# Interleaving a token-mixing stage with the projections on either side of it, on one Trainium2 core

## The chip, the cores and the metric

The program runs on one core of one Trainium2 chip. The core has TensorE (PE, matmuls), VectorE (DVE), ScalarE (ACT), GpSimd (POOL) and SyncE (SP, which only issues transfers here). Each engine runs its own instruction list in order; engines wait for one another on semaphores. The metric is the device time in microseconds of one execution; smaller is better.

## What is computed

The reference is a chain of transformer layers on 256 tokens of width 1024. The part that the change touches is the second mixer, a gated MLP that mixes tokens within chunks of 128, and the first matmuls behind it:

```python
def gmlp_mixer(h, w_in, ln_g, ln_b, ws, bs, w_out):
    z = gelu(h @ w_in)                       # 1024 -> 4096
    u, v = z[..., :2048], z[..., 2048:]
    v = layernorm(v, ln_g, ln_b)
    vc = v.reshape(B, S // 128, 128, 8, 256) # chunks of 128 tokens, 8 groups of 256 features
    mixed = einsum('gpq,bnqgc->bnpgc', ws, vc) + bs.T[None, None, :, :, None]
    return (u * mixed.reshape(B, S, 2048)) @ w_out   # 2048 -> 1024
...
x = x + g_m * o_lat
x = x + g_f * squared_relu_mlp(modulate(x, norm_ffn_g[i], sh_f, sc_f), ffn_w1[i], ffn_w2[i])
```

## The kernel before

All engines' programs are written out by hand, with hand-placed semaphore waits; nothing reorders them. Activations lie feature-major: a tile is 128 features by 256 tokens.

**Split products.** Every large product is made of three matmuls (lines 529 to 531): a number is kept as a rounded high part and the rest as a low part, and high by high, low by high and high by low are summed in PSUM. So each weight chunk (128 by 1024, 512 KB, eight 128 by 128 tiles) passes ACT, which writes `w_hi` (line 1148), and then DVE, which writes `w_lo` (line 1579). Four chunks are held in a ring: `convert(c)` on ACT waits until PE has used chunk c - 4 (`matmul_steps`), `convert(c)` on DVE waits for ACT's (`weight_hi`), and PE waits for DVE's (`weight_lo`). Activations are split likewise: DVE makes an fp32 tile in one of four slots of `tile_f32`, ACT writes `s_hi`, POOL writes `s_lo` (line 2131).

**The stages around the change**, in PE's order:

- `gm_u0` (8 chunks): the first half of u. `gm_v` (16 chunks): v, with tokens on the partitions. `gm_u1` (8 chunks, 8 groups): the second half of u. A group is the 24 matmuls that fill one PSUM bank. Banks 0 and 1 alternate; ACT's Gelu (`evacuate`, line 1163) empties each.
- During `gm_u1` DVE converts seven chunks, normalises v (`ln_mv`, `v_gm`, line 1930, semaphore `v_normed`), makes 16 bias terms of 128 by 128 (line 1924), and does four of the products that make the conditioning vectors of later layers (`modulate_loop`, line 1594).
- Mixing: for each of 16 tiles t, PE multiplies `v_gm` by `ws` (line 881) into bank 4 or 5; DVE applies gain and bias (line 1941) and multiplies by u (line 1944); ACT and POOL split the result. PE's step t waits until DVE has read tile t - 2.
- `gm_out` (16 chunks): 8 groups of 16 tiles each, banks 0 and 1. DVE adds each group into the residual x (`residual`, line 1672); ACT scales x and rounds it (`raw_tile`), DVE makes the low part (`raw_low`, line 1645), ACT squares it. `ffn1_up` begins on these tiles, and its first group needs all eight.

Of the kernel before, what the change touches and what calls it, by code (L numbers as in the profile page):

```python
# [31 lines left out]
GM = 2048  # L32
# [20 lines left out]
    ("gm_u0", [1] * 8), ("gm_v", [0, 0, 0, 2] * 4), ("gm_u1", [1] * 8), ("gm_out", [0, 1] * 8),  # L53
# [48 lines left out]
def banks_of_groups(count):  # L102
# [44 lines left out]
def build_program(nc, vecs, consts, gm_rows, c_rows, rel_ext, x_in, ctx_in, ada, weights,  # L147
# [13 lines left out]
    with hold:  # L161
# [219 lines left out]
        class Attention:  # L381
# [14 lines left out]
        ln_counted, ln_var, ln_std, v_normed, ws_sums, ws_sum_ready, mixed = (  # L396
            sem(n) for n in ("ln_counted", "ln_var", "ln_std", "v_normed", "ws_sums", "ws_sum_ready", "mixed"))
# [125 lines left out]
        def _(pe):  # L523
# [350 lines left out]
            run(project("gm_u1", 8, normed))  # L874
            pe.wait_ge(v_normed, 2)
            pe.wait_ge(ws_sum_ready, 2)
            for t in range(GM // P):
                if t >= 2:
                    pe.wait_ge(split_src, written(split0["gm_s"] + t - 2))
                for n in range(2):  # L880
                    last = pe.matmul(bank[4 + t % 2][:, n * P:(n + 1) * P], v_gm[:, n, t * P:(t + 1) * P],  # L881
                                     ws[:, t // 2, :], start=True, stop=True)
                last.then_inc(mixed, 1)
# [255 lines left out]
        def _(act):  # L1139
# [423 lines left out]
        def _(dve):  # L1563
# [356 lines left out]
            dve.wait_ge(ws_sum_ready, 2)  # L1920
            dve.wait_ge(gm_in, 32)
            for j in range(7):
                for t in range(2 * j, 2 * j + (4 if j == 6 else 2)):
                    ins = dve.scalar_tensor_tensor((bs_all if t % 2 else mix_bias)[:, t // 2, :], ws_sum[:, t // 2, :],
                                                   V("gm_ln_b", t, 1), bs_all[:, t // 2, :], ALU.mult, ALU.add)
                convert(chunk0["gm_u1"] + j + 4)
# [7 lines left out]
            then(ins)  # L1934

            def mixed_tile(t):
                i = split0["gm_s"] + t
                dst = tile_f32[:, i % 4, :].rearrange("p (n q) -> p n q", n=2)
                dve.wait_ge(mixed, t + 1)
                dve.wait_ge(split_lo, i - 3)  # L1940
                then(dve.scalar_tensor_tensor(dst, bank[4 + t % 2][:, 0:S].rearrange("p (n q) -> p n q", n=2),
                                              V("gm_ln_g", t, 1),
                                              (bs_all if t % 2 else mix_bias)[:, t // 2:t // 2 + 1, :].to_broadcast([P, 2, P]), ALU.mult, ALU.add))
                dve.tensor_tensor(tile_f32[:, i % 4, :], tile_f32[:, i % 4, :], u_gm[:, t, :],
                                  ALU.mult).then_inc(split_src, 1)
# [181 lines left out]
        def _(pool):  # L2127
# [73 lines left out]
            pool.dma_start(sq[:, 4:8, :].rearrange("p a b -> p (a b)"), gm_rows.partition_broadcast(P)).then_inc(gm_in, 16)  # L2201
            for t in range(GM // P):
# [170 lines left out]
```

## Time and profile before

| what | value |
|---|---|
| median of 3 runs | 983.95 us (978.9 to 984.32) |
| the profiled execution, its own time | 983.29 us |
| its span | 981.5 us |
| mean granted TensorE clock | 0.973 |
| busy: PE, DVE, ACT, POOL | 935.3, 707.3, 539.3, 303.9 us |

Times inside the trace count from the start of the span. A busy share is a mean over very different stages; a stage is read from its own stretch.

### The profile page before, as it was taken

To read this page: it belongs to the slowest core of one execution; us is meant where nothing else is said; L and a number is where in the kernel's file an instruction comes from. 1 tells how busy PE (TensorE), PEld (TensorE's weight loads), DVE (VectorE), ACT (ScalarE), POOL (GpSimd) and SP (SyncE) were. 2 spreads that over 40 slices of the span, in tenths; PEclk is the share of its full clock that TensorE was granted. 3 is DMA by queue.
4 is the path that set the end of the run, shared out by engine and by line. 5 is a ranking of instruction groups with operands and counts; after the bars stand their busy time and mean duration, and the time that the engine had idled before them with its cause. 6 is when DMAs were issued, how large, how long until landed. Compare 5 with 4: busy or idle time off the path is not lost.

```text
span 981.5 us, 19551 instructions
## 1 busy us (share of the span) xinstructions
PE 935.3 (95%) x6882; PEld 869.0 (89%) x6882; DVE 707.3 (72%) x1134; ACT 539.3 (55%) x922; POOL 303.9 (31%) x272
## 2 busy tenths in 40 slices
PE   5998989899999999999979999999999999999996
PEld 5877557799999999988979999999999878899996
DVE  3997679777988777897976787555555873475664
ACT  3465656565665444655635666654444762674645
POOL 1952020137997111120052288731110000330012
PEclk9798999999999999999979999999999998999998
DMA  9856185169888777788615686555665332255421
GB/s 346 292 188 228 42 230 186 51 215 317 306 274 273 288 280 278 248 317 302 224 50 187 232 282 200 187 172 192 185 194 171 108 111 84 87 174 191 151 87 43
DMA packets 57052, 195.60 MB, mean 199 GB/s; under 512 B 6303, under 2 KB 9791, under 8 KB 56736
## 3 DMA queue, kind: packets, MB, share of 16 engines
q1 hardware_dynamic: 55312, 192.36, 57.9%
q0 software_dynamic: 1680, 2.44, 1.1%
q8 instruction: 37, 0.61, 0.3%
q14 instruction: 23, 0.19, 0.1%
HBM read 192.65 MB, written 1.07 MB: 197 GB/s over the span
## 4 chain that ended last, share of the span: by engine, by line
PE 77%; DVE 14%; issue 4%; ACT 3%; DMA 1%; POOL 0%; DVEq 0%; SPq 0%; ACTq 0%
PE bank L529 23%; PE bank L530 22%; PE bank L531 22%; DVE w_lo L1579 3%; DVE ada_raw L1586 2%; ACT w_hi L1148 1%; DVE products L1681 1%; PE bank L927 1%; PE bank L953 1%; PE bank L627 1%; DVE ada_raw L1681 1%; DMA x<-x_in 1%; PE bank L826 1%; PE bank L881 1%; DVE ada_raw L1594 1%
## 5 line engine op out<-in xcount | busy, mean ns | idle before, releaser
L1579 DVE TENSOR_TENSOR w_lo<-raw,w_hi 128x1024 fp32r<-128x1024 f32 (+1 forms) x261 | 338.8, 1300 | 107.3 <-ACT w_hi L1148 104.7
L1148 ACT ACTIVATE w_hi<-raw 128x1024 fp32r<-128x1024 f32 (+1 forms) x261 | 272.4, 1045 | 173.0 <-PE bank L531 165.1
L529 PE MATMUL bank<-act_hi,w_hi 128*128 128x258 f32 (+1 forms) x872 | 249.6, 286 | 0.0
L530 PE MATMUL bank<-act_lo,w_hi 128*128 128x258 f32 (+1 forms) x872 | 246.4, 283 | 0.0
L531 PE MATMUL bank<-act_hi,w_lo 128*128 128x258 f32 (+1 forms) x872 | 246.1, 282 | 0.0
L529 PEld LDWEIGHTS bank<-act_hi,w_hi 128*128 128x128 f32 x872 | 165.6, 190 | 3.3 <-issue 2.8
L530 PEld LDWEIGHTS bank<-act_lo,w_hi 128*128 128x128 f32 x872 | 165.6, 190 | 1.0 <-issue 1.0
L531 PEld LDWEIGHTS bank<-act_hi,w_lo 128*128 128x128 f32 x872 | 165.7, 190 | 0.0
L529 PE MATMUL bank<-hid_hi,w_hi 128*128 128x256 f32 x512 | 143.9, 281 | 0.0
L530 PE MATMUL bank<-hid_lo,w_hi 128*128 128x256 f32 x512 | 143.9, 281 | 0.0
L531 PE MATMUL bank<-hid_hi,w_lo 128*128 128x256 f32 x512 | 143.9, 281 | 0.0
L531 PEld LDWEIGHTS bank<-hid_hi,w_lo 128*128 128x128 f32 x512 | 97.2, 190 | 0.0
L529 PEld LDWEIGHTS bank<-hid_hi,w_hi 128*128 128x128 f32 x512 | 97.2, 190 | 0.0
L530 PEld LDWEIGHTS bank<-hid_lo,w_hi 128*128 128x128 f32 x512 | 96.1, 188 | 0.0
L2187 POOL TENSOR_TENSOR tile_f<-relu 128x256 f32<-128x256 f32 x64 | 80.4, 1256 | 30.6 <-ACT relu L1382 30.5
L2191 POOL TENSOR_TENSOR hid_lo<-tile_f,hid_hi 128x256 f32 x64 | 75.0, 1173 | 18.0 <-POOL tile_f L2187 18.0
L2139 POOL TENSOR_TENSOR square_sum<-square_sum,sq 128x256 f32<-128x256 f32 x30 | 38.8, 1292 | 134.6 <-ACT sq L1180 134.4
L1594 DVE CUSTOM_DVE_ANT_0 ada_raw<-ada_raw,silu_row 128x1024 f32<-128x1024 f32 x56 | 75.8, 1354 | 2.3 <-DMA ada_raw<-ada 2.0
L2131 POOL TENSOR_TENSOR s_lo<-tile_f,s_hi 128x256 fp32r<-128x256 f32 x24 | 23.4, 992 | 97.8 <-ACT s_hi L1153 97.8
L529 PE MATMUL bank<-s_hi,w_hi 128*128 128x256 f32 x192 | 53.5, 279 | 0.0
L530 PE MATMUL bank<-s_lo,w_hi 128*128 128x256 f32 x192 | 53.0, 276 | 0.0
L531 PE MATMUL bank<-s_hi,w_lo 128*128 128x256 f32 x192 | 53.0, 276 | 0.0
(356 smaller groups left out, 1820.4 us busy)
## 6 DMA issues: line engine op xcount, KB each, us to landing
raw<-weights SPq DMA_DIRECT2D x247, 512.0 KB, 3.8
ada_raw<-ada SPq DMA_DIRECT2D x88, 512.0 KB, 4.9
raw<-weights SPq DMA_DIRECT2D x14, 384.0 KB, 4.7
ada_more<-ada SPq DMA_DIRECT2D x8, 512.0 KB, 6.2
bias<-bias_by_distance SPq DMA_DIRECT2D x1, 2048.0 KB, 9.3
x<-x_in SPq DMA_DIRECT2D x1, 1024.0 KB, 7.5
ctx<-ctx_in SPq DMA_DIRECT2D x1, 1024.0 KB, 9.5
out<-result SPq DMA_DIRECT2D x4, 256.0 KB, 2.7
```

The source lines that it names most:

```text
L529: pe.matmul(dst, w[0], a[0], start=start, stop=False)
L530: pe.matmul(dst, w[0], a[1], start=False, stop=False)
L531: return pe.matmul(dst, w[1], a[0], start=False, stop=stop)
L1148: act.activation(w_hi[:, slot, 0:width_of(c)], raw[:, slot, 0:width_of(c)], ACT.Copy).then_inc(weight_hi, 1)
L1579: dve.tensor_tensor(w_lo[:, slot, 0:w], raw[:, slot, 0:w], w_hi[:, slot, 0:w].bitcast(fp32), ALU.subtract).then_inc(weight_lo, 1)
L1586: dve.tensor_tensor_reduce(ada_raw[:, a % RING, :], ada_raw[:, a % RING, :], silu_row[:], 1.0, V("ada_b0", 2 * KT + a, 1), ALU.mult, ALU.a ...
L1594: dve.tensor_tensor_reduce(ada_raw[:, q, :], ada_raw[:, q, :], silu_row[:], 1.0, 0.0, ALU.mult, ALU.add, ada_col[:, q:q + 1]).then_inc(ada ...
L1681: ins = dve.tensor_tensor_reduce(dst, first_ada(o), row[:], 1.0, V("ada_b0", k, 1), ALU.mult, ALU.add, mod_in[:, k, s_:s_ + 1])
L2131: pool.tensor_tensor(lo, tile_f32[:, i % 4, :], hi.bitcast(fp32), ALU.subtract).then_inc(split_lo, 1)
L2139: pool.tensor_tensor(square_sum[:], sq[:, 0, :] if k == 1 else square_sum[:], sq[:, k, :], ALU.add).then_inc(square_sums, 1)
L2187: pool.tensor_tensor(tile_f32[:, i % 4, :], relu[:, g % 2, :], relu[:, g % 2, :], ALU.mult).then_inc(hid_squared, 1)
L2191: pool.tensor_tensor(hid_lo[:, ds(it * 8 + g, 1), :], tile_f32[:, i % 4:i % 4 + 1, :], hid_hi[:, ds(it * 8 + g, 1), :].bitcast(fp32), ALU. ...
```

## The change

PE takes up `gm_u1` in three parts: groups 0 to 3; a wait for the normalised v; then groups 4 to 7 with one mixing tile behind each. Then each of the 16 input tiles of `gm_out` is used by two output groups at once (banks 2 and 3), with the mixing of tile k + 4 behind it; mixed tiles go through banks 4 to 7. The chunks of `w_out` are stored in the order that this needs. The other six groups follow, over four banks. The split tiles are kept in slots shifted by 8, since the inputs of `gm_u1` are still in use. POOL makes 8 of the 16 bias terms; DVE makes the low parts of tiles 2, 5, 8, 11 and 14 that POOL made. ACT's and DVE's lists are rewritten to match, and the two loops of `gm_out` are written out.

```diff
-("gm_out", [0, 1] * 8),
+("gm_out", [0, 0, 1, 1] + [0, 1] * 6),
...
+            elif name == "gm_out":
+                banks.append((g + 2) % 4)
...                                          # PE
-            run(project("gm_u1", 8, normed))
+            def mix(t):
+                if t >= 4:
+                    pe.wait_ge(split_src, written(split0["gm_s"] + t - 4))
+                for n in range(2):
+                    last = pe.matmul(bank[4 + t % 4][:, n * P:(n + 1) * P], v_gm[:, n, t * P:(t + 1) * P],
+                                     ws[:, t // 2, :], start=True, stop=True)
+                last.then_inc(mixed, 1)
+            def first_out(g, k):
+                n, c = group0["gm_out"] + g, chunk0["gm_out"] + 2 * (k // 8) + g
+                if k % 8 == 0:
+                    pe.wait_ge(weight_lo, c + 1)
+                if k == 0:
+                    pe.wait_ge(evacuated, n - 3)
+                last = split_product(bank[bank_of[n]][:, 0:S], weight(c, k % 8 * P, P), mixed_s(k), k == 0, k == 15)
+                if k % 8 == 7:
+                    last.then_inc(matmul_steps, 1)
+            stage = project("gm_u1", 8, normed)
+            for g in range(4):
+                next(stage)
             pe.wait_ge(v_normed, 2)
             pe.wait_ge(ws_sum_ready, 2)
-            for t in range(GM // P):
-                if t >= 2:
-                    pe.wait_ge(split_src, written(split0["gm_s"] + t - 2))
...
+            for t in range(4):
+                next(stage)
+                mix(t)
+            run(stage)
+            for k in range(GM // P):
+                pe.wait_ge(split_lo, split0["gm_s"] + k + 1)
+                first_out(0, k)
+                first_out(1, k)
+                if k + 4 < GM // P:
+                    mix(k + 4)
+            run(project("gm_out", 16, mixed_s, locals_=range(4, 16), banks=4))
...                                          # ACT, in the loop over the groups of gm_u1
+                if g >= 4:
+                    split(split0["gm_s"] + g - 4, s_hi[:, g + 4, :])
+            for t in range(4, GM // P):
+                split(split0["gm_s"] + t, s_hi[:, (t + KT) % 16, :])
+                if t == 7:
+                    shift_columns(SHIFT3)
+                if t in (10, 12):
+                    convert(chunk0["gm_out"] + t // 2 - 1)
             act.wait_ge(gains, 3)
+            for g in range(KT):
+                raw_tile("gm_out", g, gain_column(4))
+                for c in range(chunk0["gm_out"] + 2 * g + 6, chunk0["gm_out"] + min(2 * g + 8, 20)):
+                    convert(c)
+                square_residual("gm_out", g)
...                                          # DVE
+            for j in range(8):
+                if j < 7:
+                    convert(chunk0["gm_u1"] + j + 4)
                 if j in (1, 2):
                     dve.wait_ge(ln_std, j)
                     then(dve.reciprocal(ln_mv[:, j - 1, 3:4], ln_mv[:, j - 1, 2:3]))
...
                 if j % 2 == 0:
                     modulate_loop(68 + j // 2)
+                for i in range(j - 1, KT if j == 7 else j) if j > 0 else ():
+                    dve.wait_ge(mix_bias_ready, 2 * i + 2)
+                    then(dve.scalar_tensor_tensor(bs_all[:, i, :], ws_sum[:, i, :], V("gm_ln_b", 2 * i + 1, 1),
+                                                  bs_all[:, i, :], ALU.mult, ALU.add))
+                if j >= 4:
+                    mixed_tile(j - 4)
+                if j == 7:
+                    mixed_low(2)
+            for t in range(4, GM // P):
...
                 mixed_tile(t)
+                if t > 4 and t % 3 == 0:
+                    mixed_low(t - 1)
+                if t == 4:
+                    convert(chunk0["gm_out"] + 3)
+                if t == 7:
+                    gain_of(4, mods[:, SCALE3, :], V("norm_ffn_g", KT, KT))
+                if t in (11, 13):
+                    convert(chunk0["gm_out"] + (t - 3) // 2)
             shift_low(SHIFT3, 3)
+            for g in range(KT):
+                residual("gm_out", g, mods[:, GATE2, g:g + 1])
+                raw_low(RAW["ffn1_in"], g, gain_column(4))
+                for c in range(chunk0["gm_out"] + 2 * g + 6, chunk0["gm_out"] + min(2 * g + 8, 20)):
+                    convert(c)
...                                          # POOL
+            pool.wait_ge(ws_sum_ready, 2)
+            pool.wait_ge(gm_in, 32)
+            for j in range(GM // P // 2):
+                pool.tensor_scalar(mix_bias[:, j, :], ws_sum[:, j, :], V("gm_ln_b", 2 * j, 1), None,
+                                   ALU.mult).then_inc(mix_bias_ready, 1)
+                pool.wait_ge(mix_bias_ready, 2 * j + 1)
+                pool.tensor_tensor(mix_bias[:, j, :], mix_bias[:, j, :], bs_all[:, j, :], ALU.add).then_inc(mix_bias_ready, 1)
```

**PE, the end of `gm_u1` and the mixing.** Lines 529 to 531 before are 531 to 533 after, and 881 is 885; three rows are one input tile of a group. Before:

```order
L529 MATMUL bank1<-s_hi,w_hi 128x256
L530 MATMUL bank1<-s_lo,w_hi 128x256
L531 MATMUL bank1<-s_hi,w_lo 128x256
L881 MATMUL bank4<-ws,v_gm 128x128 x2
L881 MATMUL bank5<-ws,v_gm 128x128 x2
L881 MATMUL bank4<-ws,v_gm 128x128 x2
```

After, behind the last tile of `gm_u1` (bank 1):

```order
L533 MATMUL bank1<-s_hi,w_lo 128x256
L885 MATMUL bank7<-ws,v_gm 128x128 x2
L531 MATMUL bank2<-s_hi,w_hi 128x256
L532 MATMUL bank2<-s_lo,w_hi 128x256
L533 MATMUL bank2<-s_hi,w_lo 128x256
L531 MATMUL bank3<-s_hi,w_hi 128x256
L532 MATMUL bank3<-s_lo,w_hi 128x256
L533 MATMUL bank3<-s_hi,w_lo 128x256
L885 MATMUL bank4<-ws,v_gm 128x128 x2
```

The sixteen mixing steps stood in one block; now six matmuls of `gm_out` stand between two of them.

**ACT, from group 2 of `gm_u1` on.** `u_gm` is the emptying of a group, `w_hi` a weight chunk, `s_hi` the rounding of a mixed tile. Lines 1163, 1148 and 1153 before are 1192, 1177 and 1182 after. Before:

```order
L1163 ACTIVATE u_gm<-bank0 128x256
L1148 ACTIVATE w_hi<-raw 128x1024
L1163 ACTIVATE u_gm<-bank1 128x256
L1148 ACTIVATE w_hi<-raw 128x1024
L1163 ACTIVATE u_gm<-bank0 128x256
```

After, groups 4 to 6:

```order
L1192 ACTIVATE u_gm<-bank0 128x256
L1177 ACTIVATE w_hi<-raw 128x1024
L1182 ACTIVATE s_hi<-tile_f32 128x256
L1192 ACTIVATE u_gm<-bank1 128x256
L1177 ACTIVATE w_hi<-raw 128x1024
L1182 ACTIVATE s_hi<-tile_f32 128x256
L1192 ACTIVATE u_gm<-bank0 128x256
```

A rounding of a mixed tile, made by DVE, now stands between a chunk's conversion and the emptying of the next group.

**DVE, the same place.** `w_lo` is a weight chunk, `tile_f32` the two instructions of a mixed tile, `sq<-sq,vec` a bias term. Lines 1579, 1924, 1941 and 1944 before are 1611, 1983, 1958 and 1961 after. Before, the end of `gm_u1`:

```order
L1579 TENSOR_TENSOR w_lo<-raw,w_hi 128x1024
L1924 SCALAR_TENSOR_TENSOR mix_bias<-sq,vec 128x128
L1924 SCALAR_TENSOR_TENSOR sq<-sq,vec 128x128
L1579 TENSOR_TENSOR w_lo<-raw,w_hi 128x1024
L1594 ISA ada_raw,ada_col<-ada_raw,silu_row 128x1024
```

After, from the conversion that follows group 4 of `gm_u1`:

```order
L1611 TENSOR_TENSOR w_lo<-raw,w_hi 128x1024
L1626 ISA ada_raw,ada_col<-ada_raw,silu_row 128x1024
L1626 ISA ada_col 128x1
L1983 SCALAR_TENSOR_TENSOR sq<-sq,vec 128x128
L1958 SCALAR_TENSOR_TENSOR tile_f32<-bank4,vec,mix_bias 128x256
L1961 TENSOR_TENSOR tile_f32<-tile_f32,u_gm 128x256
L1611 TENSOR_TENSOR w_lo<-raw,w_hi 128x1024
L1983 SCALAR_TENSOR_TENSOR sq<-sq,vec 128x128
L1958 SCALAR_TENSOR_TENSOR tile_f32<-bank5,vec,sq 128x256
```

A mixed tile now stands behind a conversion, and the next conversion behind the tile; bank4 and bank5 are the first two of the four mixing banks.

**DVE, the last groups of `gm_out`.** `x` is the residual, `act_lo` the low part for `ffn1_up`. After, one group of the last seven:

```order
L1704 SCALAR_TENSOR_TENSOR x<-bank0,mods,x 128x256
L1677 SCALAR_TENSOR_TENSOR act_lo<-x,gain,act_hi 128x256
L1611 TENSOR_TENSOR w_lo<-raw,w_hi 128x1024 x2
```

Before, one conversion stood ahead of each residual and one behind it; now both stand behind one group's residual and ahead of the next one's.

## Rows read from the trace of the kernel before

**Rows 1.** The page, busy time of each engine.

```profile
PE 935.3 (95%) x6882; PEld 869.0 (89%) x6882; DVE 707.3 (72%) x1134; ACT 539.3 (55%) x922; POOL 303.9 (31%) x272
```

**Rows 2.** Busy time by stretch: most of `gm_u1`, then the mixing.

```profile
core 0: us, PE busy (x) PEld busy (x) DVE busy (x) ACT busy (x) POOL busy (x), PEclk, DMA share, GB/s
...
468.50:488.30 19.80, 19.80 (x177) 19.80 (x177) 18.92 (x37) 12.27 (x18) 0.00 (x0) 1.00 0.63 212
488.30:509.50 21.20, 14.47 (x78) 12.25 (x77) 19.18 (x41) 7.83 (x19) 13.22 (x15) 0.76 0.24 78
```

**Rows 3.** Timeline of PE's weight loads: start, length, what, idle before.

```profile
488.15 0.97 PEld L881 LDWEIGHTS bank<-ws,v_gm 128*128 128x128 f32 x8
492.56 1.78 PEld L881 LDWEIGHTS bank<-ws,v_gm 128*128 128x128 f32 x8 [3.44 <-DVE tile_f L1944]
...
508.01 0.19 PEld L529 LDWEIGHTS bank<-s_hi,w_hi 128*128 128x128 f32 x1
```

**Rows 4.** Waits, 440 to 570 us: total, times, longest.

```profile
PEld bank L881 <- DVE tile_f L1944: 8.9, 10, 3.4
```

**Rows 5.** Timeline of DVE in `gm_u1` and in the mixing.

```profile
474.67 0.34 DVE L1924 SCALAR_TENSOR_TENSOR sq<-sq,vec 128x128 f32<-128x128 f32 x1
474.93 1.21 DVE L1579 TENSOR_TENSOR w_lo<-raw,w_hi 128x1024 fp32r<-128x1024 f32 x1
...
479.37 1.35 DVE L1930 TENSOR_SCALAR v_gm<-v_gm,ln_mv 128x2048 f32<-128x2048 f32 x1
480.64 1.22 DVE L1594 CUSTOM_DVE_ANT_0 ada_raw<-ada_raw,silu_row 128x1024 f32<-128x1024 f32 x1
...
493.28 1.76 DVE L1579 TENSOR_TENSOR w_lo<-raw,w_hi 128x1024 fp32r<-128x1024 f32 x1
...
506.57 0.48 DVE L1941 SCALAR_TENSOR_TENSOR tile_f<-bank,vec,sq 128x256 f32<-128x256 f32 x1
...
507.45 0.48 DVE L1941 SCALAR_TENSOR_TENSOR tile_f<-bank,vec,mix_bias 128x256 f32<-128x256 f32 x1
...
509.24 0.71 DVE L1609 SCALAR_TENSOR_TENSOR gain<-mods,vec 128x8 f32<-128x8 f32 x1
```

**Rows 6.** Timeline of ACT in `gm_u1` and in the mixing.

```profile
476.58 0.39 ACT L1163 ACTIVATE u_gm<-bank 128x256 f32<-128x256 f32 x1
476.86 1.05 ACT L1148 ACTIVATE w_hi<-raw 128x1024 fp32r<-128x1024 f32 x1
477.81 0.37 ACT L1163 ACTIVATE u_gm<-bank 128x256 f32<-128x256 f32 x1
...
492.54 0.42 ACT L1153 ACTIVATE s_hi<-tile_f 128x256 fp32r<-128x256 f32 x1 [2.65 <-DVE tile_f L1944]
```

**Rows 7.** Timeline of POOL in the mixing.

```profile
493.04 2.58 POOL L2131 TENSOR_TENSOR s_lo<-tile_f,s_hi 128x256 fp32r<-128x256 f32 x2 [65.51 <-ACT s_hi L1153]
...
503.67 6.96 POOL L2131 TENSOR_TENSOR s_lo<-tile_f,s_hi 128x256 fp32r<-128x256 f32 x8 [0.81 <-ACT s_hi L1153]
```

**Rows 8.** Timeline of PE at the start of `ffn1_up`.

```profile
551.66 0.28 PE L529 MATMUL bank<-act_hi,w_hi 128*128 128x258 f32 x1
...
554.20 0.39 PE L529 MATMUL bank<-act_hi,w_hi 128*128 128x258 f32 x1
```

**Rows 9.** Timeline of DVE at the same place.

```profile
552.16 0.48 DVE L1672 SCALAR_TENSOR_TENSOR x<-bank,mods,x 128x256 f32 x1 [0.31 <-PE bank L531]
553.66 0.48 DVE L1645 SCALAR_TENSOR_TENSOR act_lo<-x,gain,act_hi  x1 [1.01 <-ACT act_hi L1174]
```

**Rows 10.** Busy time by stretch, around an earlier gap of PE (columns as in Rows 2).

```profile
90.00:93.00 3.00, 0.30 (x3) 0.21 (x2) 2.98 (x4) 1.03 (x2) 3.00 (x2) 0.91 0.93 369
93.00:95.00 2.00, 1.97 (x9) 1.97 (x10) 1.92 (x4) 0.07 (x1) 0.92 (x2) 0.50 1.01 361
...
99.00:101.00 2.00, 2.00 (x9) 1.59 (x9) 0.00 (x0) 0.13 (x1) 0.00 (x0) 0.93 0.47 193
```

**Rows 11.** Busy time by stretch, inside the mixing.

```profile
496.00:500.00 4.00, 3.66 (x15) 3.37 (x16) 2.97 (x7) 1.60 (x4) 2.76 (x4) 0.50 0.39 131
```

More of the change, by code:

```diff
@@ L52 @@
     ("ffn0_up", [1] * 32), ("ffn0_down", [0, 0, 0, 1] * 8),
-    ("gm_u0", [1] * 8), ("gm_v", [0, 0, 0, 2] * 4), ("gm_u1", [1] * 8), ("gm_out", [0, 1] * 8),
+    ("gm_u0", [1] * 8), ("gm_v", [0, 0, 0, 2] * 4), ("gm_u1", [1] * 8), ("gm_out", [0, 0, 1, 1] + [0, 1] * 6),
     ("ffn1_up", [1] * 32), ("ffn1_down", [0, 0, 0, 1] * 8),
@@ L873, in _, with mixed_s @@
                           stop=True).then_inc(ws_sums, 1)
-            run(project("gm_u1", 8, normed))
+            def mixed_s(k):
+                return s_hi[:, (k + KT) % 16, :], s_lo[:, (k + KT) % 16, :]
+            def mix(t):
[5 more added lines that the diff above has]
+                last.then_inc(mixed, 1)
@@ L875, in _ @@
+            for g in range(4):
+                next(stage)
             pe.wait_ge(v_normed, 2)
             pe.wait_ge(ws_sum_ready, 2)
-            for t in range(GM // P):
-                if t >= 2:
-                    pe.wait_ge(split_src, written(split0["gm_s"] + t - 2))
[L880 to L883, printed above, removed]
@@ L884, in _ @@
-            with pe.Fori(0, 2) as it:
-                run(project("gm_out", 16, lambda k: (s_hi[:, k, :], s_lo[:, k, :]), locals_=range(8),
-                            it=it, per=4, a_wait=lambda k: split0["gm_s"] + k + 1))
+            for t in range(4):
[8 more added lines that the diff above has]
+                    mix(k + 4)
@@ L1919, in _, with mixed_tile, mixed_low @@
                 dve.bn_aggr(ln_mv[:, tt, 0:2], ln_stats[:, tt, :, :]).then_inc(ln_var, 1)
[L1920 to L1926, printed above, removed]
+            def mixed_tile(t):
+                i = split0["gm_s"] + t
+                dst = tile_f32[:, i % 4, :].rearrange("p (n q) -> p n q", n=2)
+                dve.wait_ge(mixed, t + 1)
+                dve.wait_ge(split_lo, i - 3)
+                then(dve.scalar_tensor_tensor(dst, bank[4 + t % 4][:, 0:S].rearrange("p (n q) -> p n q", n=2),
+                                              V("gm_ln_g", t, 1),
+                                              (bs_all if t % 2 else mix_bias)[:, t // 2:t // 2 + 1, :].to_broadcast([P, 2, P]), ALU.mult, ALU.add))
+                dve.tensor_tensor(tile_f32[:, i % 4, :], tile_f32[:, i % 4, :], u_gm[:, t, :],
+                                  ALU.mult).then_inc(split_src, 1)
+            def mixed_low(t):
+                i = split0["gm_s"] + t
+                dve.wait_ge(split_hi, i + 1)
+                dve.wait_ge(split_lo, i)
+                dve.tensor_tensor(s_lo[:, (t + KT) % 16, :], tile_f32[:, i % 4, :], s_hi[:, (t + KT) % 16, :].bitcast(fp32),
+                                  ALU.subtract).then_inc(split_lo, 1)
+            for j in range(8):
+                if j < 7:
+                    convert(chunk0["gm_u1"] + j + 4)
                 if j in (1, 2):
@@ L1933, in _ @@
                     modulate_loop(68 + j // 2)
[L1934 to L1945, printed above, removed]
@@ L2335 @@
         chunks_of(a["ffn_w1"][0]), chunks_of(a["ffn_w2"][0]),
[L2336 removed]
+        chunks_of(gm_in[:, :GM // 2]), chunks_by_token(gm_in[:, GM:], 512), chunks_of(gm_in[:, GM // 2:GM]),
+        chunks_of(a["gm_w_out"][0])[[0, 2, 1, 3, *range(4, 16)]],
         chunks_of(a["ffn_w1"][1]), chunks_of(a["ffn_w2"][1]),
```

36 lines of the change are left out of this document (9 added, 27 removed).

## The prediction

> **What bounds the kernel now.** I read the page first: PE is busy 95% of the span [rows 1], so the kernel is a matmul stream, and only a place where that stream breaks can give time back. The table by stretch finds it: in `gm_u1` PE is busy all of the time at full clock, with DVE busy 18.92 of 19.8 us; in the mixing PE is busy 14.47 of 21.2 us at a mean clock of 0.76 [rows 2]. The timeline shows the edges: mixing starts at 488.15, `gm_out` at 508.01 [rows 3]. PE's own work there is small. Eight weight loads took 0.97 us at full clock, 0.11 each between starts, so the 64 take 7.1 us. The stretch is 19.9 us long, so **12.7 us** is what perfect hiding would return. The waits name the holder: PE waited 8.9 us on DVE's mixed tile [rows 4], and the rest is low clock.
>
> Who sets the pace is DVE: a mixed tile takes 0.88 us, from 506.57 to 507.45 [rows 5], 14 us for 16, and the timeline of DVE is nearly solid in `gm_u1` too. So the question is not whether PE can interleave, but whether DVE, ACT and POOL reach the same point earlier.
>
> **The change, part by part.**
>
> *PE's order.* No matmul is added. From 508.01 to 551.66 PE does 384 matmuls, 0.1137 us each [rows 3, 8]: a group of 24 is 2.73 us, one input tile for two groups 0.68, a mixing tile 0.45. Before, the first two output groups ended at 508.01 + 32 tiles x 0.341 = **518.9**. The last six groups, 32.8 us, are unchanged. The sum is therefore: when do the first two groups end now, and is the seam to `ffn1_up` as tight?
>
> *The new wait for v.* Group 3 of `gm_u1` ends four groups ahead of 488.15, at 477.2. PE now waits there for the normalised v, which DVE finished at 479.37 + 1.35 = 480.7 [rows 5]; before, PE did groups 4 to 7 meanwhile. The removed bias terms do not bring it forward: the conversion ahead of it on DVE waits for ACT's `w_hi`, which ended at 477.91 because two table loads for the square root had held ACT until 476.58 [rows 6]; 477.9 + 1.2 + 0.2 + 1.35 is 480.7 again. So PE stands idle 3.5 us, and all that follows group 4 waits behind it. What this idling does to the clock can be read elsewhere: after a gap of 2.7 us at 90.3 the granted clock was 0.50 (1.2 of 2.4 GHz) from 93 on and nearly full again only in the slice 99 to 101, though PE was busy all of that time [rows 10]. If it is low for all of group 4, the group takes 5.4 us in place of 2.7; if for none, 2.7. I take 2.0 us lost, nearer to the row: group 4 ends at 485.4.
>
> The Trainium skill, "TensorE: Matmul & The Clock Gate", section "What's actually happening", says that the array falls to half rate after idling and rises again after sustained activity; the trace agrees [rows 10]. With no such rule the sum would be 2.0 us lower here.
>
> *ACT and DVE in lock-step.* This is the heart of it. ACT's list is now: empty group g, convert a chunk, round mixed tile g - 4, empty group g + 1. DVE's is: convert that chunk, bias term, mixed tile. Each waits for the other once per group: DVE's conversion for ACT's, ACT's rounding for the mixed tile that stands behind that conversion, and ACT's next emptying and conversion stand behind the rounding. Nothing overlaps. Durations: emptying 0.28, `w_hi` 0.95 from start to start [rows 6], `w_lo` 1.2, conditioning product 1.2, bias term 0.26 plus a wait on itself, say 0.35, mixed tile 0.88 [rows 5], rounding 0.42 [rows 6]; 0.05 to 0.15 for a handover.
> - from the end of group 4 to mixed tile 0: 0.15 + 0.28 + 0.95 + 1.2 + 1.2 + 0.35 + 0.88 = 5.0
> - to tile 1: 0.42 + 0.28 + 0.95 + 1.2 + 0.35 + 0.88 + 0.1 = 4.2
> - to tile 2 (a conditioning product and its addition too): 5.6
> - to tile 3 (two bias terms, no conversion): 1.6, and the low part of tile 2: 0.4.
>
> Sum 16.8, so DVE is through at 502.2. PE has long done groups 4 to 7 and the first two input tiles (at about 497) and waits for tile 2's low part.
>
> *Tiles 4 to 15.* DVE: 12 mixed tiles 10.6, three low parts 1.2, the gain 0.7 [rows 5], three conversions. Those lie beside POOL's subtractions, where one took 1.76 in place of 1.21 [rows 5, 7]; 1.2 to 1.76 each, I take 1.5, so 4.5. Two of them wait for ACT's rounding and `w_hi` (1.4 us after the tile, of which a tile or more is covered): 0.8. Together 17.8: tile 15 at 520.0. Then rounding 0.42, POOL's subtraction 0.87 (6.96 for 8) [rows 7], PE's last tile pair 0.68 and handovers: **522.2**, against 518.9: +3.3. PE's own work per tile, 0.68 + 0.45 = 1.13, is under DVE's 1.5 at full clock but 2.26 at half; PE's second idling, some 5 us, may bring that for a few tiles: 0 to 2.5, I take 0.5, since DVE has slack against it only in part.
>
> *Moved to POOL:* 16 instructions of 128 by 128, beside DVE's work until about 477. They hide, if they are half as long as the 0.87 of a 128 by 256 one, because the first is needed at 477 and the last at 500. What DVE pays beside them is a rival, below.
>
> *The seam.* Before, `ffn1_up` began at 551.66 and its eighth input tile at 554.20; DVE's low part ended at 553.66 + 0.48 = 554.14 [rows 8, 9], so the seam was just tight and without slack. Now, after the last group, ACT converts chunk 19 (0.15 + 0.95), DVE converts it (1.2), and only then comes the residual 0.48, ACT's scaling (0.5), the low part 0.49, handovers 0.3: 4.1 us in place of 2.5. Nothing hides this **1.6 us**. Between 0 and 3.3, the upper end if this gap costs clock as well.
>
> *Nothing else.* Loads run ahead: a chunk's slot is freed by DVE's conversion as before. Four banks for the last six groups remove no wait, since PE had none. The written-out loops cost nothing beside a full PE.
>
> Sum: 3.3 + 0.5 + 1.6 = **+5.4 us** on the profiled execution's 983.29, hence 988.7, I say **989**. The median of the runs, 983.95, stands 0.7 above that execution, which is below what a measurement tells.
>
> **The rivals.**
>
> *The engines keep up (faster).* If ACT and DVE slipped past each other, PE would return all of the 12.7 us but the tail of the tiles: 970.6. For it: 8 bias terms leave DVE (2.1 us) and four mixed tiles start before 488. Against it: both lists are fixed, and DVE was busy 18.92 of 19.8 and 19.18 of 21.2 us already [rows 2]. It needs the three rounds to take under 3 us each, and their parts add to over 4. 8%.
>
> *POOL blocks DVE.* A conversion beside POOL took 1.76, not 1.21, and POOL's two took 2.58, not 1.74 [rows 5, 7]. Five such DVE instructions stand before v is normalised; at 0.55 each the wait for v grows by up to 2.7, the tail's conversions add 0.8: 992. 15%. The Trainium skill, "SBUF — State Buffer", section "Who interferes with whom", says that a DVE instruction with two SBUF inputs and a GpSimd instruction that reads SBUF exclude each other, the later one blocking fully; that speaks against moving the bias terms. The trace agrees as far as those two rows go.
>
> *The clock stays low (slower).* In the mixing the clock was 0.50 while PE was busy 3.66 of 4 us [rows 11]. PE's work from group 4 to the end of the first two output groups is 4 x 2.73 + 16 x 1.13 = 29.0 us; all at half rate it would end at 480.7 + 58 = 538.7, +19.8, with the seam 1004.7. Over 1% is reached when some 9 us more than I count are at half rate. Against it: groups 4 to 7 are dense, and in [rows 10] a dense stretch was back at full by 101. 12%, at about 1000 on average.
>
> *The stage is level.* No clock cost and short conversions: 988.7 - 2.5 - 0.9 - 0.5 = 985. 15%. My forecast holds 50%.
>
> **How the numbers follow.** 1% of this kernel, about what a measurement tells from no change, is 9.8 us. The forecast with its bounds spans 985 to 995; faster by over 1% comes from the first rival alone, 8%; slower by over 1% takes 11 of the low clock's 12% and 3% from the tops of the POOL case and of my own, 14%; the rest, 78%, is within 1%. The range leaves out most of the first rival and the upper half of the third: 980 to 998.
>
> **What would show it.** PE idle about 3.5 us at 477, ended by DVE's `v_gm`, and a second gap of some 5 us near 497, ended by DVE's `s_lo`; ACT waiting for DVE's mixed tile, and DVE for `w_hi`, three times each with over 1 us; a granted clock of 0.5 behind both gaps; first residual of `gm_out` near 522; a gap of 1.6 us in the first group of `ffn1_up`. If PE shows no gap at 477, or the first residual comes before 515, the argument is wrong.

## The result, and the profile after

| | kernel before | changed kernel |
|---|---|---|
| median of 20 runs | 983.94 us | 987.25 us |
| lowest to highest | 978.90 to 987.65 | 984.54 to 990.89 |
| the profiled execution, and its span | 983.29, 981.5 | 987.11, 985.3 |
| mean granted clock | 0.973 | 0.975 |

The ratio is **1.0035, 95% [1.0023, 1.0048]**: about 3.4 us slower. The forecast was 989 and level with before (within 1%), from a sum of +5.4. Two executions that took far longer than the others of their kernel, 1038.95 us of "three" and 1820.55 us of "both" (names as below), are left out of all ratios.

The page's line of busy time, to be laid beside [rows 1]:

```profile
PE 935.2 (95%) x6882; PEld 869.4 (88%) x6882; DVE 705.3 (72%) x1131; ACT 538.9 (55%) x922; POOL 316.4 (32%) x283
```

Only POOL's share moved (+12.5 us); a whole page does not show what happened. The stretches do. These are the two of [rows 2] and the one behind them:

```profile
468.50:488.30 19.80, 16.34 (x121) 16.14 (x120) 14.65 (x22) 9.60 (x14) 15.78 (x16) 0.83 0.56 186
488.30:509.50 21.20, 16.63 (x132) 16.44 (x131) 17.20 (x35) 7.10 (x15) 4.40 (x6) 0.92 0.31 100
509.50:520.00 10.50, 8.44 (x68) 7.79 (x67) 9.71 (x18) 4.42 (x9) 3.91 (x5) 1.00 0.16 52
```

In the second stretch PE does more than before (x132 for x78, clock 0.92 for 0.76): the overlap is real. It is paid for in the first, where PE was full and now misses 3.5 us and much of its clock, and DVE, once busy 18.92 us, does only 14.65. The stretch of mixing is not removed but spread out.

PE's timeline shows the places where it stood still, with the releaser:

```profile
480.51 0.58 PE L531 MATMUL bank<-s_hi,w_hi 128*128 128x256 f32 x1 [3.46 <-DVE v_gm L1977]
502.91 0.43 PE L531 MATMUL bank<-s_hi,w_hi 128*128 128x256 f32 x1 [4.57 <-DVE s_lo L1968]
514.20 0.39 PE L531 MATMUL bank<-s_hi,w_hi 128*128 128x256 f32 x1 [0.18 <-POOL s_lo L2176]
516.60 0.39 PE L531 MATMUL bank<-s_hi,w_hi 128*128 128x256 f32 x1 [0.99 <-DVE s_lo L1968]
519.61 0.39 PE L531 MATMUL bank<-s_hi,w_hi 128*128 128x256 f32 x1 [0.89 <-POOL s_lo L2176]
521.08 0.39 PE L531 MATMUL bank<-s_hi,w_hi 128*128 128x256 f32 x1 [0.50 <-DVE s_lo L1968]
...
559.61 0.39 PE L531 MATMUL bank<-act_hi,w_hi 128*128 128x258 f32 x1 [1.42 <-DVE act_lo L1677]
560.07 0.60 PE L615 MATMUL bank<-square_sum,mean 128*128 128x256 f32 x2
```

The first, the second and the last before `square_sum` are the three that were forecast. Two stretches of the same kernel, in the columns of [rows 2], show the clock behind the first two:

```profile
479.60:486.40 6.80, 5.89 (x29) 5.90 (x30) 4.30 (x6) 0.37 (x2) 5.18 (x5) 0.53 0.49 154
503.50:507.00 3.50, 3.50 (x21) 3.50 (x19) 3.43 (x7) 0.83 (x2) 1.49 (x2) 0.57 0.17 41
```

ACT's timeline from group 4 on, where `s_hi` is the rounding of a mixed tile:

```profile
486.03 0.38 ACT L1192 ACTIVATE u_gm<-bank 128x256 f32<-128x256 f32 x1 [7.40 <-PE bank L533]
486.31 1.05 ACT L1177 ACTIVATE w_hi<-raw 128x1024 fp32r<-128x1024 f32 x1
491.11 0.42 ACT L1182 ACTIVATE s_hi<-tile_f 128x256 fp32r<-128x256 f32 x1 [3.75 <-DVE tile_f L1961]
...
495.29 0.42 ACT L1182 ACTIVATE s_hi<-tile_f 128x256 fp32r<-128x256 f32 x1 [2.53 <-DVE tile_f L1961]
...
500.92 0.42 ACT L1182 ACTIVATE s_hi<-tile_f 128x256 fp32r<-128x256 f32 x1 [4.00 <-DVE tile_f L1961]
```

And DVE's, over the same rounds, then in the later tiles and behind them:

```profile
487.47 1.23 DVE L1611 TENSOR_TENSOR w_lo<-raw,w_hi 128x1024 fp32r<-128x1024 f32 x1 [3.53 <-ACT w_hi L1177]
...
490.66 0.42 DVE L1961 TENSOR_TENSOR tile_f<-tile_f,u_gm 128x256 f32<-128x256 f32 x1
492.79 1.22 DVE L1611 TENSOR_TENSOR w_lo<-raw,w_hi 128x1024 fp32r<-128x1024 f32 x1 [1.71 <-ACT w_hi L1177]
...
496.96 1.23 DVE L1611 TENSOR_TENSOR w_lo<-raw,w_hi 128x1024 fp32r<-128x1024 f32 x1 [1.70 <-ACT w_hi L1177]
...
503.29 0.85 DVE L1961 TENSOR_TENSOR tile_f<-tile_f,u_gm 128x256 f32<-128x256 f32 x1
504.06 1.21 DVE L1611 TENSOR_TENSOR w_lo<-raw,w_hi 128x1024 fp32r<-128x1024 f32 x1
...
508.54 0.15 DVE L1641 SCALAR_TENSOR_TENSOR gain<-mods,vec 128x8 f32<-128x8 f32 x1
...
522.74 0.48 DVE L1704 SCALAR_TENSOR_TENSOR x<-bank,mods,x 128x256 f32<-128x256 f32 x1 [1.63 <-PE bank L533]
```

Read the two together: ACT waits for DVE 3.75, 2.53 and 4.00 us, DVE for ACT 3.53, 1.71 and 1.70, in turns. The first of DVE's, 3.53, comes from PE's first gap: ACT itself had waited 7.40 us for group 4. The other two are the lock-step; no single row of waits shows it, since each engine is the other's releaser.

**The stage as a measure.** Below, a kernel's *stage* is the time from the first of the small `ws` by `ones` matmuls, just ahead of `gm_u1`, to the sum of squares at the end of the first group of `ffn1_up`. It is 464.77 to 554.66 before, 89.89 us, and 464.27 to 560.07 after, **95.80**: +5.91. The *seam*, from the first matmul of `ffn1_up` to that sum, is 3.00 before and 4.55 after. All code around the stage is unchanged. Behind it the two profiled executions differ too, before and after:

```profile
554.66:981.50 426.84, 412.68 (x3264) 394.37 (x3262) 262.10 (x469) 235.19 (x426) 111.57 (x105) 0.98 0.48 155
```

```profile
560.07:985.30 425.23, 411.23 (x3264) 392.70 (x3262) 261.14 (x468) 234.40 (x425) 112.11 (x105) 0.98 0.49 154
```

The same 3264 matmuls took 1.6 us less after. A stage is read from one execution, and the code behind it, which no edit touches, took 423.9 to 429.6 us in the kernels below. So a stage tells where an edit acts, to about 1 us; the ratio of many runs tells what it is worth. Stages compare best among the variants of the changed kernel: in ten of these eleven the ratio says 0.7 to 3.8 us less than the stage's difference from 89.89 does. A part of that is that the profiled execution before, 983.29 us, lay 0.7 to 1.3 below the medians of its kernel; the rest is open.

### The profile page after: what moved, and what is told of

Read it like the earlier page. It is cut to its first block, busy times and chain, and to the rows that moved or that the text cites. A ratio compares the mean times of both kernels' runs of the same rounds, so it can differ in the third digit from the quotient of the medians.

```text
span 985.3 us, 19447 instructions
## 1 busy us (share of the span) xinstructions
PE 935.2 (95%) x6882; PEld 869.4 (88%) x6882; DVE 705.3 (72%) x1131; ACT 538.9 (55%) x922; POOL 316.4 (32%) x283
## 4 chain that ended last, share of the span: by engine, by line
PE 76%; DVE 14%; ACT 4%; issue 4%; DMA 1%; POOL 0%; SPq 0%; DVEq 0%; ACTq 0%; POOLq 0%
PE bank L531 23%; PE bank L532 22%; PE bank L533 22%; DVE w_lo L1611 2%; DVE ada_raw L1618 2%; ACT w_hi L1177 2%; DVE products L1713 1%; PE bank L629 1%; PE bank L956 1%; PE bank L982 1%; DVE ada_raw L1713 1%; DMA x<-x_in 1%; PE bank L828 1%; DVE ada_more L1713 1%; DVE tile_f L1958 1%
## 5 line engine op out<-in xcount | busy, mean ns | idle before, releaser
L531 PE MATMUL bank<-s_hi,w_hi 128*128 128x256 f32 x192 | 57.1, 297 | 10.6 <-DVE s_lo L1968 6.1
L531 PEld LDWEIGHTS bank<-s_hi,w_hi 128*128 128x128 f32 x192 | 37.6, 196 | 12.3 <-DVE s_lo L1968 6.6
```

The source lines that it names most:

```text
L531: pe.matmul(dst, w[0], a[0], start=start, stop=False)
```

## The experiments

Each ratio is to the kernel before, from the number of runs that the table gives; expectations stand as written before the run. All results first:

| kernel | what it is | stage, us | runs | ratio [95%] |
|---|---|---|---|---|
| changed | | 95.80 | 20 | 1.0035 [1.0023, 1.0048] |
| seam | old order at the seam | 92.98 | 12 | 1.0014 [0.9991, 1.0037] |
| late wait | v awaited behind group 4 | 92.78 | 12 | 1.0022 [1.0004, 1.0039] |
| unlock | ACT's roundings a group later | 92.38 | 12 | 1.0006 [0.9987, 1.0026] |
| three | these three | 88.42 | 11 | 0.9969 [0.9952, 0.9987] |
| low parts | three, and POOL makes all low parts | 86.65 | 12 | 0.9971 [0.9953, 0.9990] |
| DVE's bias | changed, DVE makes all bias terms | 98.66 | 6 | 1.0051 [1.0031, 1.0071] |
| late products | three, and two products and the gain behind tile 15 | 85.64 | 5 | 0.9938 [0.9917, 0.9958] |
| both | low parts and late products | | 6 | 0.9939 [0.9916, 0.9961] |
| late conversions | both, and two conversions behind tile 15 | 84.01 | 6 | **0.9931** [0.9908, 0.9954] |
| after u | changed, but all mixing after `gm_u1` | 91.50 | 12 | 0.9992 [0.9976, 1.0008] |
| after u, mended | after u, seam, late products | 86.03 | 9 | 0.9936 [0.9916, 0.9956] |
| bias alone | before, POOL makes 8 bias terms | 90.51 | 12 | 1.0005 [0.9990, 1.0020] |

**Seam.** The order of conversions and residuals of the kernel before, in ACT's and DVE's loops:

```diff
-for c in range(chunk0["gm_out"] + 2 * g + 6, chunk0["gm_out"] + min(2 * g + 8, 20)):
+for c in range(chunk0["gm_out"] + max(2 * g + 5, 6), chunk0["gm_out"] + 2 * g + (7 if g < 7 else 6)):
```

> The changed kernel with one edit: in the last groups of gm_out each residual again stands between two conversions on DVE and ACT, as before the change, and not behind both. Theory (the seam is a wait of its own, made by the order): the gap of 1.43 us in the first group of ffn1_up goes, the time falls by 1.4 us against the changed kernel, so it is 2.0 us above the kernel before (ratio 1.002). Rival (the gap is only the lateness of the last group, or it is given back in ffn1_up, where DVE and ACT then run late anyway): the gap stays, or the time stays at 1.0035.

The seam came back from 4.55 to 2.86 and PE's gap went: the 1.4 us at 559.61 are the conversion that stands ahead of the last residual. The stage fell by 2.8, more than this; 1.1 of it is the first gap, where the clock in this execution was low for half as long (0.76 on average from 480 to 487, against 0.57 in the changed kernel), though nothing there was edited.

**Late wait.**

```diff
-for g in range(4):
+for g in range(5):
     next(stage)
 pe.wait_ge(v_normed, 2)
...
 for t in range(4):
-    next(stage)
+    if t > 0:
+        next(stage)
     mix(t)
```

> The changed kernel with one edit: PE's wait for the normalised v stands behind group 4 of gm_u1 in place of ahead of it; the matmuls keep their order. Theory (all behind group 4 is a chain, and the wait pushes it): PE's gap at 477 shrinks from 3.46 to under 1 us, the clock stays at 1.0 there, ACT's w_hi for the chunk behind group 4 begins near 481 in place of 486.3, and DVE's idle of 3.53 us ahead of its conversion goes; DVE's own work behind v lasts until 483.9, so the chain moves by 3.5 us: time 3.5 us under the changed kernel, ratio 1.000 to the kernel before. Rival (DVE is full and the idle PE time costs nothing): no change, 1.0035.

PE's timeline:

```profile
481.26 0.71 PE L885 MATMUL bank<-ws,v_gm 128*128 128x128 f32 x4 [0.74 <-DVE v_gm L1978]
489.53 0.36 PE L531 MATMUL bank<-s_hi,w_hi 128*128 128x256 f32 x1 [1.01 <-ACT u_gm L1193]
500.48 0.58 PE L531 MATMUL bank<-s_hi,w_hi 128*128 128x256 f32 x1 [4.84 <-DVE s_lo L1969]
```

The wait shrank from 3.46 to 0.74 and the clock stayed full (479.6 to 486.4: 1.00 for 0.53). Of the 5.4 us that PE won, the stage kept 3.0. A new wait shows where the rest went: PE now stands for ACT, which empties a bank (`u_gm`) only after a rounding that waited 6.81 us for DVE:

```profile
488.70 0.42 ACT L1183 ACTIVATE s_hi<-tile_f 128x256 fp32r<-128x256 f32 x1 [6.81 <-DVE tile_f L1962]
```

The lock-step, not PE, then sets the pace.

**Unlock.** In ACT's list only, the rounding of tile g - 4 moves behind the next group:

```diff
-if g >= 4:
-    split(split0["gm_s"] + g - 4, s_hi[:, g + 4, :])
-for t in range(4, GM // P):
+if g >= 5:
+    split(split0["gm_s"] + g - 5, s_hi[:, g + 3, :])
+for t in range(3, GM // P):
```

> The changed kernel with one edit: on ACT each rounding of a mixed tile stands one group later, behind the emptying and the conversion of that next group. Theory (ACT and DVE are in lock-step for three rounds): DVE's idle of 1.71 and 1.70 us ahead of its conversions goes, the first low part that PE waits for at 502.9 comes 3.4 us earlier, and the time falls by 3.4 us, ratio 1.000. Rival (DVE's own work sets the pace, the waits are covered later): the waits move to other places and the time stays at 1.0035.

DVE's three waits of 3.53, 1.71 and 1.70 became one of 2.67, PE's second gap fell from 4.57 to 2.1, the stage by 3.4. Not all of the 3.4 is the lists. The clock behind the first gap was again low for a shorter time in this execution (0.76 from 480 to 487), so ACT emptied group 4 20.9 us behind the stage's start and not 21.8: 0.9 us of luck. And of the 3.4 us of waits that went, 1.0 came back, because DVE's instructions now stood beside POOL's (rows of the two engines' timelines, in order of time):

```profile
491.11 1.21 POOL L2176 TENSOR_TENSOR s_lo<-tile_f,s_hi 128x256 fp32r<-128x256 f32 x1 [5.80 <-ACT s_hi L1182]
491.63 0.83 DVE L1983 SCALAR_TENSOR_TENSOR sq<-sq,vec 128x128 f32<-128x128 f32 x1
494.04 1.15 POOL L2176 TENSOR_TENSOR s_lo<-tile_f,s_hi 128x256 fp32r<-128x256 f32 x1 [1.72 <-ACT s_hi L1182]
494.50 1.77 DVE L1626 CUSTOM_DVE_ANT_0 ada_raw<-ada_raw,silu_row 128x1024 f32<-128x1024 f32 x1
```

In the changed kernel the same two took 0.34 and 1.22. No instruction was removed: moving three roundings in one short list was worth about 2.5 us.

**Three.**

> All three edits together: the late wait, the roundings one group later, the old order at the seam. Theory: DVE works from 480.4 without its idle times of 3.53 + 1.71 + 1.70 us, so tile 15 is ready 6.9 us earlier; with the seam the time is 8.3 us under the changed kernel, ratio 0.995. What is then late next is DVE's own work for tiles 4 to 15. Rival (the three cover each other): no more than the best of the three alone, ratio 1.000 or above.

The stage fell by 7.4 and the kernel is now faster than before by 0.3%. Singly the three gave 2.8, 3.0 and 3.4; without the 1.1 and 0.9 us of clock in the first and the last that is 7.2, so they add up, and to more than the 5.9 that the change had cost. But 88.42 is little below the 89.89 of before: PE still waited up to 3.2 us at a time for DVE's low part.

**Low parts.** In "three", DVE's five `mixed_low` calls go and POOL's loop makes all sixteen.

> The three edits together, and one more: the five low parts that the change gave to DVE go back to POOL. The stretch from the ones-by-ws matmuls to the sum of squares in ffn1_up took 88.4 us with the three edits, 95.8 in the changed kernel and 89.9 before. Theory (DVE's own work is what is late next): DVE loses five subtractions of 0.34 us, and PE's wait for the low part of tile 2, 3.2 us, shrinks by 0.7 more, because POOL makes it while DVE goes on: the stretch takes 86.5 to 87, time 1.5 us less, ratio 0.995. Rival (POOL is slow and blocks DVE: a multiply took 0.85 us in place of 0.42 beside it six times): DVE's multiplies lengthen by as much as the subtractions gave, and the stretch stays at 88.4.

The stage fell by 1.8, as expected; the ratio did not move. Giving DVE these parts was no gain, and its cost is below what the runs can tell.

**DVE's bias.** In the changed kernel POOL's loop goes and DVE makes a second term each time:

```diff
-dve.wait_ge(mix_bias_ready, 2 * i + 2)
+dve.scalar_tensor_tensor(mix_bias[:, i, :], ws_sum[:, i, :], V("gm_ln_b", 2 * i, 1),
+                         bs_all[:, i, :], ALU.mult, ALU.add)
```

> The changed kernel with one edit: DVE makes all 16 bias terms again, POOL none. Theory (DVE waited 3.53 us ahead of the chunk behind group 4, so work ahead of that is free, and only the five terms behind it count): the stretch grows from 95.8 by 5 x 0.26 = 1.3 us less what DVE's instructions were lengthened beside POOL, so 96 to 97; ratio 1.004. v is ready at the same 16.2 us, since DVE waits there for ACT. Rival (POOL blocks DVE, the 15% case of the prediction): v is ready 1 to 3 us earlier and the stretch shrinks to 93 to 95.

PE's gaps were 3.20 and 5.62 us:

```profile
481.04 0.58 PE L531 MATMUL bank<-s_hi,w_hi 128*128 128x256 f32 x1 [3.20 <-DVE v_gm L1979]
504.74 0.58 PE L531 MATMUL bank<-s_hi,w_hi 128*128 128x256 f32 x1 [5.62 <-DVE s_lo L1970]
```

So v was awaited hardly less long without POOL's work, and the second gap grew by a full 1.05 us. The stage was longer by 2.9, of which 1.3 is the odd spacing told of at the end; the two ratios' intervals overlap, and the profiled execution, 995.08 us, was the slowest of six (median 989.76). So no run shows that POOL's share of the bias terms hurts this kernel; that it helps is likely by the second gap and not settled by the ratios. In the changed kernel v was ready 16.18 us behind the start of the stage, here 15.93: POOL's interference there costs a quarter of a microsecond.

**Late products.** In "three", DVE's last two conditioning products and the gain, which nothing before `ffn1_up` needs, go behind tile 15:

```diff
-if j % 2 == 0:
+if j in (0, 2):
     modulate_loop(68 + j // 2)
...
-if t == 7:
-    gain_of(4, mods[:, SCALE3, :], V("norm_ffn_g", KT, KT))
...
+modulate_loop(70)
+modulate_loop(71)
+gain_of(4, mods[:, SCALE3, :], V("norm_ffn_g", KT, KT))
```

> The three edits together, and one more: the last two conditioning products of 1.2 us each, and the gain made from them, stand behind tile 15 in place of among the groups of gm_u1. Theory (DVE is the bound up to tile 15): all mixed tiles come 2.4 us earlier, PE's wait for the low part of tile 2 goes from 3.2 to about 0.8 us, and behind tile 15 the products cost nothing, since DVE waited 1.6 us there and PE has four banks: the stretch takes 86 us, ratio 0.994. Rival (they only move): the first residual and the chunk behind it come too late, PE waits in gm_out for w_lo, and the stretch stays near 88.4.

PE's timeline, its first three gaps:

```profile
480.61 0.71 PE L885 MATMUL bank<-ws,v_gm 128*128 128x128 f32 x4 [0.76 <-DVE v_gm L1978]
494.57 0.38 PE L531 MATMUL bank<-s_hi,w_hi 128*128 128x256 f32 x1 [1.42 <-DVE s_lo L1969]
497.58 0.39 PE L531 MATMUL bank<-s_hi,w_hi 128*128 128x256 f32 x1 [0.47 <-POOL s_lo L2178]
```

No gap is over 1.42 us, and the clock is full throughout the mixing:

```profile
488.30:509.50 21.20, 18.21 (x149) 17.20 (x147) 20.03 (x38) 8.97 (x19) 7.37 (x10) 1.00 0.32 105
```

Here work is moved out of the way on the engine that bounds the stage, and it pays at once: 2.8 us of stage, 0.3% of time.

**Both, and late conversions.** "Both" joins "low parts" and "late products"; its profiled execution is the one left out, so only its ratio counts: 0.9939 where 0.992 was expected, which its interval still holds. Then DVE's conversions of chunks 4 and 5 of `w_out` go behind tile 15 too:

> The three edits with the low parts on POOL and the two products behind tile 15. Theory: both gains add, stretch 84.5 us, ratio 0.992; what is late then is DVE's 0.88 us for each mixed tile with two conversions between them, against 1.13 us of PE per tile, so PE's waits are under 2 us in all and the next bound is PE itself. Rival: the gains overlap, 86 us or more.

> The kernel with all five edits (three edits, low parts on POOL, two products behind tile 15), and DVE's two conversions among tiles 11 to 13 moved behind tile 15 as well. The stretch from the ones-by-ws matmuls to the sum of squares was 85.6 us with four of them. Theory (DVE is the bound to tile 15): tile 15 comes 2 x 1.2 + 0.6 us earlier, the stretch is 82 to 83.5 us, ratio 0.991. Rival (PE or the ring is the bound by now): PE waits for the two chunks behind the first two groups, or the mixed tiles run into PE's 1.13 us per tile, and the stretch stays at 85 or above, ratio 0.994.

```diff
-if t in (11, 13):
-    convert(chunk0["gm_out"] + (t - 3) // 2)
+for c in (4, 5):
+    convert(chunk0["gm_out"] + c)
```

PE's timeline of the last kernel:

```profile
511.28 0.39 PE L531 MATMUL bank<-s_hi,w_hi 128*128 128x256 f32 x1 [1.03 <-POOL s_lo L2174]
518.47 0.39 PE L531 MATMUL bank<-s_hi,w_hi 128*128 128x256 f32 x1 [0.79 <-DVE w_lo L1612]
```

Another 1.6 us of stage against "late products", for two edits (the low parts are one of them), but the ratios of the three kernels lie within one another's intervals. The second row is the rival's: late conversions now come late for PE. This is the fastest kernel of the study, **0.7%** under the kernel before.

**After u.** Is the early start worth anything? PE does all of `gm_u1`, then four mixing tiles, then goes on as in the changed kernel:

```diff
-for g in range(4):
-    next(stage)
+run(stage)
 pe.wait_ge(v_normed, 2)
 pe.wait_ge(ws_sum_ready, 2)
 for t in range(4):
-    next(stage)
     mix(t)
-run(stage)
```

> The changed kernel without its first part: PE does all of gm_u1, then mixing tiles 0 to 3, then the two output groups among the other mixed tiles; ACT and DVE take up the mixed tiles behind gm_u1 too. Theory (the start among the groups of u bought nothing, for DVE is the bound and the lock-step cost it 7 us): no gap at 477, DVE is through gm_u1 near 491 and through tile 15 near 513, against 509.2 before and 520.3 in the changed kernel; the stretch of 95.8 us becomes 87.5 plus or minus 1, and that is less than the 89.9 before: ratio 0.998. Rival (the early start is worth something and only the waits spoil it): 91 us or more.

> The one before with the old order at the seam and the two conditioning products behind tile 15, to stand beside the kernel with the early start and the same edits, 85.6 us and ratio 0.994. Theory: DVE's list has the same instructions in nearly the same places, so the stretch is the same to 1 us, 85 to 86.5 us: the early start itself is worth nothing. Rival: the early start lets DVE work while PE finishes gm_u1, and without it the stretch is 88 us or more.

```profile
494.32 0.58 PE L531 MATMUL bank<-s_hi,w_hi 128*128 128x256 f32 x1 [5.00 <-POOL s_lo L2167]
```

One large gap of 5.00 us in place of two, and the kernel is level with before, 0.4% better than the changed one. The stage of "after u" was 91.5 where 87.5 was expected, the figure that the rival had named. Of the 4 us, 1.3 is the odd spacing told of at the end, and 2.6 that DVE was through tile 15 50.8 us behind the stage's start in place of 48.2; 1.7 of it was there at the end of `gm_u1`. So "after u" by itself does not decide, and the mended pair has to. With the seam and the late products mended, "after u" reaches 86.03 and 0.9936, "late products", which starts early, 85.64 and 0.9938. **No gain from the early start shows**: 0.4 us by the stages, less than nothing if the odd spacing (1.3 us, in "after u, mended") is taken off, and nothing by the ratios, whose intervals reach 2 us either way. The interleaving of `gm_out` with the mixing is another matter: both kernels have it, and no run takes it out. Nor was "late products" tried on the kernel before, so how much of the 0.6% is the interleaving and how much DVE's shorter list stays open. The nearest figure is "three", where nothing is moved behind tile 15: 0.3% under the kernel before.

**Bias alone.** The kernel before, with eight bias terms made by POOL as in the changed kernel:

> The kernel before with one part of the change alone: POOL makes 8 of the 16 bias terms. Theory (DVE was the bound before too; what stood ahead of mixed tile 0 counts): DVE sheds 8 x 0.26 us and pays about 0.1 us for each of the others, so tile 0 comes 1 to 1.5 us earlier, the stretch of 89.9 us becomes 88.5 to 89, ratio 0.999. Rival (POOL blocks DVE by what it takes over): 90 us or more.

No change (1.0005), and the stage did not shrink as expected. The same two stretches as [rows 2], the second one:

```profile
488.30:509.50 21.20, 15.12 (x80) 13.34 (x79) 18.87 (x37) 7.56 (x17) 11.00 (x13) 0.68 0.36 119
```

The clock there was 0.68 for 0.76, a longer low stretch on an unchanged order of PE, which may hide what DVE gained. The profiled execution, 988.48 us, was the slowest of the twelve (median 984.39), so its stage is a poor witness, and that the clock took the gain is argued, not shown. What the runs show is that the shift of bias terms changed the time by no more than 0.2% here.

## Why the prediction was right, and where it was off

**Right in the mechanism.** PE's three forecast gaps came where and as long as said: 3.46 for 3.5 by `v_gm`, 4.57 for "some 5" by `s_lo`, 1.42 for 1.6 at the seam. Each cause was then removed by itself and the stage fell (late wait 3.0, unlock 3.4 and seam 2.8, the last two with about 1 us of clock in each).

**The lock-step.** Its rounds were summed from rows of before. From the end of group 4 to tile 0, then to tiles 1, 2 and 3, it said 5.0, 4.2, 5.6 and 1.6. Measured, from 0.15 ahead of `u_gm` at 486.03: 5.2 (491.08), 4.2 (495.25), 5.6 (500.88), 1.6 (502.5). The sum put DVE through tile 3 and the low part of tile 2 at 502.2, and it was 502.8.

**The clock behind the first gap: under-sized.** "I take 2.0 us lost". Group 4 ran from 480.51 to some 485.9, 5.4 us for 2.73, so 2.7 were lost: the upper end. The Trainium skill's "TensorE: Matmul & The Clock Gate", section "What's actually happening", has the array at half rate after idling; the trace agrees here, at 0.53 over 479.6 to 486.4.

**Tiles 4 to 15: right in sum, wrong in parts.** 17.8 us were forecast, 17.9 measured (502.8 to 520.7). But the three conversions took 1.21 to 1.23 each, not "1.5", and the gain 0.15, not 0.7: the 0.71 of [rows 5] was stretched by POOL's eight subtractions beside it. What made up for both is that four multiplications took 0.85 in place of 0.42 (one is the row at 503.29) and one 0.98: 2.3 us that the sum did not have. Each of the five began up to 0.2 us behind the start of a subtraction of POOL's, as those at 503.11 and 509.21; where DVE's began first, at 513.13, it took 0.42, and POOL's subtraction of 513.29 took 0.85 for 0.74. So the sum had the contention with the wrong instructions, and that it came out right is luck.

**The rival "POOL blocks DVE" fell in its main part.** It had 15% and 992, for a wait for v grown by up to 2.7 and 0.8 on the tail's conversions. The tail did pay, with the 2.3 us above, but on multiplications. POOL's terms ran far longer than the "until about 477" of the text:

```profile
467.18 1.71 POOL L2250 TENSOR_SCALAR mix_bias<-sq,vec 128x128 f32<-128x128 f32 x1 [40.15 <-ACT sq L1461]
...
472.62 2.64 POOL L2250 TENSOR_SCALAR mix_bias<-sq,vec 128x128 f32<-128x128 f32 x1
...
484.49 0.46 POOL L2253 TENSOR_TENSOR mix_bias<-mix_bias,sq 128x128 f32<-128x128 f32 x1
```

Yet it was mostly POOL that was held up (2.64 against 0.60 when alone), and v came only 0.2 us later. With "DVE's bias" the stage became longer, not shorter. The Trainium skill's "SBUF — State Buffer", section "Who interferes with whom", says that a DVE instruction with two SBUF inputs and a GpSimd one that reads SBUF exclude each other, and that the order of issue decides who blocks. The rows at 503.29 (0.85 for 0.42 on DVE) and 472.62 agree. But no run here shows that moving the bias terms cost time.

**The seam.** 1.6 forecast, +1.55 measured, no clock cost.

**The sum.** The stage gave +5.9 for +5.4, and the ratio says +3.4 [2.3, 4.7]. In the profiled execution the stage began 0.5 us earlier and unchanged code behind it took 1.6 less, which makes the +3.8 from 983.29 to 987.11. So +5.4 is right for the stage and about 2 us too large for the time, outside the ratio's interval, and why the runs show less than the stage is not shown. That 989 lies only 1.8 from 987.25 is in part luck: its base lay 0.7 below the runs' median.

**"The engines keep up"** (8%, 970.6) fell for the change as it stands. The text's reason, fixed lists, was the right one, and it cuts both ways: with the lists reordered the changed kernel came to 6 to 7 us under the kernel before, with the early start or without it. What could not be had is the rest, since DVE is busy 20.03 of 21.2 us even in "late products", from 488.3 to 509.5.

## What to carry to other kernels

Before PE's work is interleaved, count what the feeding engine must do before the last tile: here that was DVE, and the early start bought nothing that shows, while three items moved behind DVE's last tile bought 2.8 us. Where two engines run fixed lists and each feeds the other, lay one round of both side by side, and put each hand-over one round late. And when loops are written anew, look at their last turn: a conversion ahead of the last residual cost 1.4 us at the seam.

## What the runs showed of the hardware

**The clock's loss varies for the same gap.** Behind a gap of about 3.5 us at the same place, the changed kernel was at 0.57 on average from 480 to 487, and "seam" and "unlock", whose code up to there is the same, at 0.76: about 1 us of difference. Gaps of 1.42 us and less in "late products" cost no clock.

**Dense matmuls were not equally dense.** From 528 to 546 the same 128 by 256 matmuls run without a gap and at clock 1.00, in the kernel before and in "after u":

```profile
528.00:546.00 18.00, 18.00 (x162) 18.00 (x161) 13.03 (x14) 8.72 (x13) 5.43 (x4) 1.00 0.56 179
```

```profile
528.00:546.00 18.00, 18.00 (x156) 18.00 (x155) 10.59 (x13) 9.06 (x13) 4.41 (x3) 1.00 0.64 219
```

The starts of weight loads are 0.1133 us apart in the first and 0.1177 in the second, over the whole of the last six groups: 288 times 0.0044 is 1.3 us. "After u, mended" and "DVE's bias" show 0.1177 too, all other kernels of the table that have a stage 0.1133. None of these edits touches PE's instructions of that stretch. It makes 1.3 of the 4 us by which "after u" missed its expected stage, and part of the 2.9 of "DVE's bias"; its own cause was not looked for and stays open.
